# The first norm, the RG-LRU phase, the compressed scores and the S5 preparation of a two-block fp32 model, in another order

## The chip, the cores and the metric

The program runs on one core of a Trainium2 chip. The metric is the device time of one execution in microseconds (us). An execution is one launch that computes both blocks of the model for one sequence of 256 tokens.

## The reference, cut to what matters

Two model blocks of width 1024 are computed in fp32. The first is an RG-LRU layer with its feed-forward layer, then a sparse-attention (NSA) layer with its own. The second is a feed-forward layer, an S5 layer, two feed-forward layers around it and a block attention (MoBA) layer. The parts that the change touches:

```python
def rmsnorm(x, g):
    return x * lax.rsqrt(jnp.mean(x * x, axis=-1, keepdims=True) + EPS) * g

def rglru_mixer(h, ...):               # 1536 channels, T = 256
    u = h @ w_in
    xb, yb = u[..., :D_RNN], u[..., D_RNN:]
    xc = conv(xb, conv_w, width 4, causal) + conv_b
    r = sigmoid(blockdiag(xc, w_ra) + b_ra)
    i = sigmoid(blockdiag(xc, w_ix) + b_ix)
    log_a = -8 * r * softplus(-lam)
    a = exp(log_a); mult = sqrt(-expm1(2 * log_a))
    h_t = a_t * h_(t-1) + mult * i * xc   # scan over the 256 tokens
    return (hs * gelu(yb)) @ w_out

# NSA: scores of 16 heads (4 per key group) on the 15 compressed keys of each group
s_c = einsum('tghd,cgd->tghc', q, kc)
p_c = masked_softmax(s_c, mask_c)

# S5: tables from lam^k, B and C, which depend on no activation
y = einsum over (chunk kernel K, powers times B, powers times C)
```

## The kernel before

Everything is one instruction stream per engine, written out by hand. TensorE (PE) takes part in all of it: activations are held transposed, channels on partitions and the 256 tokens in the free dimension, and each weight matrix arrives in **halves** of 128x1024 (128x1408 in the down projections of the feed-forward layers). A half passes four engines:

- SP loads two halves at a time from HBM into one of 4 buffers `raw`.
- ACT copies a half to `w_hi`, a rounded version (`split_hi`, L846). It runs 4 halves ahead of PE (`SPLIT = 4`), because there are 4 buffers, and waits until PE has used the old one.
- DVE makes `w_lo = raw - w_hi` (`split_lo`, L1237).
- PE multiplies in three passes (L1970 to L1972), or in two wide ones (L1976, L1977) in the down and output projections.

The activations are split the same way into `hg_hi` (ACT, L849) and `hg_lo` (DVE, L1242). The norm's factor is applied behind the product: squares are summed, one PE product with a matrix of ones gives the mean (`mean_square`, L1989), ACT takes the root (L855) and DVE the reciprocal (L1247).

Each engine works through its own queue in order, and what stands where is set by tables of slots. In the RG-LRU phase slot `j` is one half of the input projection (24 halves: 0 to 11 give `xb`, 12 to 23 give `y`). The 1536 channels are worked in 4 groups `g` of 3 tiles. For each group come the convolution (`conv`, DVE, L1468 and L1470), the gates (PE, L2117), then sigmoids, exp, tanh and sqrt (ACT, L970 to L990, with three table loads) and the recurrence (DVE, L1489 to L1497). The tables `CONV_AT`, `GATES_AT`, `RECUR_AT` and `FINISH_AT` say in which slot each group's piece is written into each engine's queue, always behind that slot's own split. The gelu of `y` (ACT, L1006) follows a rule in the loop.

In the feed-forward phases slots 0 to 10 are pairs of hidden tiles (4 halves each) and slots 11 to 18 are the 8 tiles of the down projection (2 halves each). PE starts down tile `m` when tile `m - 2` has been added to `h` (`h_written`, L1264). Two feed-forward phases of the first block also carry the preparation of the S5 tables, in 8 portions of three pieces each. C makes `cp_s` (DVE, L1318 to L1322). K is PE's 16 small products L2097, which wait for it. B makes `ba_s` (DVE, L1332 to L1336). `C_AT`, `K_AT` and `B_AT` give the slots, first for the feed-forward phase at 181 to 383 us, then for the one at 640 to 838 us. ACT issues their DMAs: `s_ca`, `c_raw` and `b_raw` with K, and `s_ba`, `b_rows` and 8 times `l_rows` in the slot behind B.

```python
for j in range(2 * RT):                    # ACT, RG-LRU
    split_hi(half0 + j + SPLIT)
    ...
    if j in GATES_AT:
        gates(GATES_AT.index(j))           # sigmoids, exp, tanh, sqrt of group g
```

Of the kernel before, what the change touches and what calls it, by code (L numbers as in the profile page):

```python
# [31 lines left out]
ALU = mybir.AluOpType  # L32
# [6 lines left out]
P = 128  # L39
# [122 lines left out]
def two_blocks(nc, ins, out, phases):  # L162
# [4 lines left out]
    with ExitStack() as ctx:  # L167
# [74 lines left out]
        x_in = sem("x_in")  # L242
# [111 lines left out]
        kc_s = na.sb("kc_s", [P, NG * NC])  # L354
# [49 lines left out]
        gates_made = sem("gates_made")  # L404
        sc_done = sem("sc_done")
# [190 lines left out]
        def _(sp):  # L596
            def load(unit, it=0, row_step=0):
# [5 lines left out]
                src = ins[kind]  # L603
                if row_step:
# [29 lines left out]
        def _(pool):  # L634
# [176 lines left out]
            sum_squares(0, lambda m: pool.wait_ge(x_in, 16))  # L811
# [20 lines left out]
        def _(act):  # L832
            act.dma_start(vec[:, :], ins["vec"]).then_inc(consts_in, 16)
            act.dma_start(h[:, :, :], ins["x"]).then_inc(x_in, 16)


            def split_hi(half, it=0):
# [5 lines left out]
                act.wait_ge(raw_loaded[r], 16 * (half // (2 * RAW) + 1) + 16 * it)  # L843
# [115 lines left out]
            def rglru_phase(ph):  # L959
                half0 = 2 * ph["u0"]  # L960

                def gates(g):


                    r, i, rt = r_s[g % 2], i_s[g % 2], root_s[g % 2]
# [6 lines left out]
                    for q in range(GT):  # L972
                        n = GT + q
                        act.activation(i[:, q, :], bank[5 + n // 2][:, n % 2 * T:(n % 2 + 1) * T], ACT.Sigmoid,
                                       bias=gain("b_ix", GT * g + q)).then_inc(sigm_made, 1)
                    if g == 0:
                        act.wait_ge(sp4_made, 1)
# [20 lines left out]
                for j in range(2 * RT):  # L998
                    split_hi(half0 + j + SPLIT)
                    if j == 1:  # L1000
                        root(ph["norm"])
                    if j > RT and j % 2:
                        u = (j - RT) // 2
# [3 lines left out]
                    if j in GATES_AT:  # L1007
                        gates(GATES_AT.index(j))
# [48 lines left out]
            def nsa_phase(ph):  # L1057
# [7 lines left out]
                for j in range(52):  # L1065
# [15 lines left out]
                    if j >= 34 and j < 50 and j % 2:  # L1081
                        u = (j - 34) // 2
                        act.wait_ge(proj_read, base + 11 + u + 1)
                        act.activation(qr_s[0:96, 2 * u:2 * u + 2, :], q_s[0:96, 2 * u:2 * u + 2, :], ACT.Copy).then_inc(q_copied, 1)
                act.wait_ge(gate_lin, 2)
# [115 lines left out]
            act.wait_ge(x_in, 16)  # L1201
            act.wait_ge(consts_in, 16)
            for m in range(KT):
                make_hg_hi(phases[0]["gain"], m)
                if m == 0:
                    split_hi(0)
            for half in range(1, SPLIT):
                split_hi(half)
# [20 lines left out]
        def _(dve):  # L1229
# [206 lines left out]
            def softplus_lambda():  # L1436
# [19 lines left out]
            def rglru_phase(ph):  # L1456
                half0 = 2 * ph["u0"]

                def conv(g):

                    slot = GT * (g % 2)
                    for j in range(4):
                        for q in range(GT):
# [3 lines left out]
                            if j == 0:  # L1467
                                last = dve.tensor_scalar(o, x, gain("conv_0", m), gain("conv_b", m), ALU.mult, ALU.add)  # L1468
                            else:
                                last = dve.scalar_tensor_tensor(o, x, gain(f"conv_{j}", m), o, ALU.mult, ALU.add)  # L1470
# [34 lines left out]
                for j in range(2 * RT):  # L1505
                    split_lo(half0 + j + SPLIT)
                    if j == 1:
                        invert(ph["norm"])
                    if j < RT and j % 2:
# [104 lines left out]
            def nsa_phase(ph):  # L1614
# [23 lines left out]
                for j in range(52):  # L1638
# [48 lines left out]
                    if j == 38:  # L1687
                        dve.wait_ge(cmp_done, 1)
                        dve.tensor_copy(kc_s[0:96, :], bank[7][0:96, 0:NG * NC]).then_inc(cmp_kept, 1)
# [22 lines left out]
                for b in range(2):  # L1712
# [1010 lines left out]
```

## Time and profile before

| | before |
|---|---|
| time, median of 3 runs | 1889.27 us |
| lowest, highest | 1884.92, 1890.38 us |
| the profiled execution, timed | 1885.09 us |
| its span, first to last instruction | 1883.1 us |
| mean granted TensorE clock | 0.970 |
| PE busy | 1766.4 us (94%) |
| DVE busy | 1336.6 us (71%) |
| ACT busy | 857.2 us (46%) |
| POOL busy | 356.8 us (19%) |

The span is 2.0 us shorter than the time of the same execution. PE is busy for 94% of it, so what can be won or lost lies in the 117 us in which PE stands still, and in stretches in which its clock is at half speed. A queue entry of another engine matters only where PE waits for it.

### The profile page before, as it was taken

To read this page: it belongs to the slowest core of one execution; us is meant where nothing else is said; L and a number is where in the kernel's file an instruction comes from. 1 tells how busy PE (TensorE), PEld (TensorE's weight loads), DVE (VectorE), ACT (ScalarE), POOL (GpSimd) and SP (SyncE) were. 2 spreads that over 40 slices of the span, in tenths; PEclk is the share of its full clock that TensorE was granted. 3 is DMA by queue.
4 is the path that set the end of the run, shared out by engine and by line. 5 is a ranking of instruction groups with operands and counts; after the bars stand their busy time and mean duration, and the time that the engine had idled before them with its cause. 6 is when DMAs were issued, how large, how long until landed. Compare 5 with 4: busy or idle time off the path is not lost. (4 is left out here: it accounts for less than half of the span.)

```text
span 1883.1 us, 32526 instructions
## 1 busy us (share of the span) xinstructions
PE 1766.4 (94%) x13218; PEld 1673.2 (89%) x13218; DVE 1336.6 (71%) x1691; ACT 857.2 (46%) x1118; POOL 356.8 (19%) x327
## 2 busy tenths in 40 slices
PE   6959999997987999979999999999999999989999
PEld 6858998797976999869998888999899989879998
DVE  7877878788567777887875766666666665586663
ACT  4755444344346444434445325544354444355442
POOL 3223000206620300142002213000300035530000
PEclk9989999998979999999999999999999999999999
DMA  7225558456410467854564543556445644425561
GB/s 283 89 91 182 207 188 284 161 172 206 146 46 1 162 229 241 283 172 148 178 229 151 213 138 133 178 180 220 159 160 187 219 154 170 161 74 176 185 233 48
DMA packets 60795, 321.89 MB, mean 171 GB/s; under 512 B 7440, under 2 KB 20304, under 8 KB 30352
## 3 DMA queue, kind: packets, MB, share of 16 engines
q1 hardware_dynamic: 37296, 286.47, 42.9%
q10 hardware_dynamic: 18864, 21.74, 3.7%
q0 software_dynamic: 4528, 12.19, 1.9%
q8 instruction: 75, 1.23, 0.3%
q14 instruction: 32, 0.26, 0.0%
HBM read 309.16 MB, written 10.09 MB: 170 GB/s over the span
## 5 line engine op out<-in xcount | busy, mean ns | idle before, releaser
L1237 DVE TENSOR_TENSOR w_lo<-raw,w_hi 128x1024 fp32r<-128x1024 f32 (+2 forms) x516 | 683.8, 1330 | 332.0 <-ACT w_hi L846 330.6
L846 ACT ACTIVATE w_hi<-raw 128x1024 fp32r<-128x1024 f32 (+2 forms) x516 | 561.3, 1095 | 687.9 <-PE bank L1972 399.5
L1970 PE MATMUL bank<-hg_hi,w_hi 128*128 128x256 f32 (+1 forms) x2672 | 768.7, 288 | 41.0 <-DVE w_lo L1237 22.7
L1971 PE MATMUL bank<-hg_lo,w_hi 128*128 128x256 f32 (+1 forms) x2672 | 760.5, 285 | 0.0
L1972 PE MATMUL bank<-hg_hi,w_lo 128*128 128x256 f32 (+1 forms) x2672 | 760.4, 285 | 0.0
L1970 PEld LDWEIGHTS bank<-hg_hi,w_hi 128*128 128x128 f32 (+1 forms) x2672 | 514.4, 193 | 49.9 <-issue 16.5
L1971 PEld LDWEIGHTS bank<-hg_lo,w_hi 128*128 128x128 f32 (+1 forms) x2672 | 515.0, 193 | 0.3
L1972 PEld LDWEIGHTS bank<-hg_hi,w_lo 128*128 128x128 f32 (+1 forms) x2672 | 514.8, 193 | 0.0
L1976 PE MATMUL bank<-hid,w_hi 128*128 128x512 f32 x1056 | 375.2, 397 | 0.6 <-DVE hid L1388 0.4
L1977 PE MATMUL bank<-hid,w_lo 128*128 128x256 f32 x1056 | 300.1, 284 | 0.0
L1976 PEld LDWEIGHTS bank<-hid,w_hi 128*128 128x128 f32 x1056 | 200.1, 190 | 48.1 <-issue 1.0
L1977 PEld LDWEIGHTS bank<-hid,w_lo 128*128 128x128 f32 x1056 | 200.3, 190 | 0.0
L649 POOL TENSOR_TENSOR sumsq<-h 128x256 f32<-128x256 f32 x11 | 10.1, 915 | 879.8 <-DVE h L1264 868.2
L652 POOL TENSOR_TENSOR square<-h 128x256 f32<-128x256 f32 x77 | 87.3, 1134 | 227.9 <-DVE h L1264 226.9
L655 POOL TENSOR_TENSOR sumsq<-sumsq,square 128x256 f32<-128x256 f32 x77 | 90.2, 1172 | 6.0
L1242 DVE SCALAR_TENSOR_TENSOR hg_lo<-h,vec,hg_hi 128x256 fp32r<-128x256 f32 x80 | 67.1, 845 | 15.9 <-ACT hg_hi L849 15.9
L891 ACT ACTIVATE hid<-hid_f 128x512 fp32r<-128x512 f32 (+1 forms) x66 | 41.8, 633 | 59.9 <-DVE hid_f L1384 59.9
L887 ACT ACTIVATE silu_s<-gate_s 128x512 f32<-128x512 f32 x66 | 41.2, 624 | 60.3 <-DVE gate_s L1377 60.3
L1261 DVE SCALAR_TENSOR_TENSOR h<-bank,h 128x256 f32<-128x256 f32 x80 | 33.6, 420 | 48.5 <-PE bank L1977 48.1
L1381 DVE TENSOR_TENSOR up_s<-bank,rstd 128x512 f32<-128x512 f32 x66 | 45.4, 688 | 19.8 <-PE bank L1972 19.8
L1377 DVE TENSOR_TENSOR gate_s<-bank,rstd 128x512 f32<-128x512 f32 x66 | 45.4, 688 | 16.8 <-PE bank L1972 16.6
L849 ACT ACTIVATE hg_hi<-h,vec 128x256 fp32r<-128x256 f32 x80 | 39.6, 503 | 25.5 <-DVE h L1264 15.0
(377 smaller groups left out, 2017.7 us busy)
## 6 DMA issues: line engine op xcount, KB each, us to landing
raw<-in_w SPq DMA_DIRECT2D x187, 1024.0 KB, 4.8
raw<-in_w SPq DMA_DIRECT2D x48, 1408.0 KB, 6.1
raw<-in_q SPq DMA_DIRECT2D x14, 768.0 KB, 4.3
raw<-in_w SPq DMA_DIRECT2D x8, 768.0 KB, 4.2
b_rows<-in_s_b_rows ACTq DMA_DIRECT2D x8, 512.0 KB, 5.1
l_rows<-s_powers ACTq DMA_DIRECT2D x64, 64.0 KB, 6.0
s_ca<-cp_s ACTq DMA_DIRECT2D x8, 512.0 KB, 4.2
s_ba<-ba_s ACTq DMA_DIRECT2D x8, 512.0 KB, 3.0
```

The costliest lines, as they stand in the source:

```text
L652: pool.tensor_tensor(square[:, :], h[:, m, :], h[:, m, :], ALU.mult).then_inc(sq_step, 1)
L655: last = pool.tensor_tensor(sumsq[:, :], sumsq[:, :], square[:, :], ALU.add)
L846: act.activation(w_hi[s][:, 0:n], raw[r][:, c * n:(c + 1) * n], ACT.Copy).then_inc(hi_made, 1)
L1237: dve.tensor_tensor(w_lo[s][:, 0:n], raw[r][:, c * n:(c + 1) * n], w_hi[s][:, 0:n].bitcast(F32), ALU.subtract).then_inc(lo_made, 1)
L1242: dve.scalar_tensor_tensor(hg_lo[:, m, :], h[:, m, :], gain(gain_name, m), hg_hi[:, m, :].bitcast(F32), ALU.mult, ALU.subtract).then_inc(h ...
L1377: dve.tensor_tensor(two(gate_s[:, :]), two(gate[:, :]), twice(rstd), ALU.mult).then_inc(gate_scaled, 1)
L1381: dve.tensor_tensor(two(up_s[:, :]), two(up[:, :]), twice(rstd), ALU.mult).then_inc(up_scaled, 1)
L1970: pe.matmul(psum, w_hi_ap, x_hi_ap, start=first, stop=False, **kw)
L1971: pe.matmul(psum, w_hi_ap, x_lo_ap, start=False, stop=False, **kw)
L1972: return pe.matmul(psum, w_lo_ap, x_hi_ap, start=False, stop=last, **kw)
L1976: pe.matmul(psum[:, :].rearrange("p (a t) -> p a t", a=2), w_hi_ap, x_pair, start=first, stop=False)
L1977: return pe.matmul(psum[:, 0:T], w_lo_ap, x_pair[:, 0, :], start=False, stop=last)
```

## The change

1. **Start.** `vec` (all per-channel constants) is loaded first on SP's queue and no longer on ACT's. `x` and the first weight unit come in two parts each. ACT makes `w_hi` of half 0 ahead of the 8 `hg_hi`. The squares for the first norm are two ACT instructions into `y_gelu` instead of 15 POOL instructions, and PE sums them in 8 products instead of 1. The norm's root and reciprocal are written one slot earlier. DVE computes `softplus(-lam)` in two parts: the first ahead of everything else, the second in slot 2.
2. **RG-LRU.** The convolution's first tap goes from DVE to ACT (`first_tap`, slots `TAP_AT`), which needs no table. ACT's gate work is cut in two: `sigmoids` in the gates' slot and `decays` (exp, tanh, sqrt) one slot later. All tables of slots are new.
3. **Compressed scores.** 32 products with the queries as weights (N = 15) become 8 with the keys as weights (32 columns, N = 512, the four groups in the four column quarters of the array). Two ACT copies and 8 transposes follow.
4. **S5 preparation.** `C_AT`, `K_AT` and `B_AT` are new.

```diff
-CONV_AT = (3, 5, 10, 12)
-GATES_AT = (7, 10, 12, 15)
-RECUR_AT = (10, 12, 15, 21)
+TAP_AT = (3, 5, 9, 11)
+CONV_AT = (4, 6, 10, 12)
+GATES_AT = (6, 8, 12, 14)
+RECUR_AT = (11, 13, 16, 18)
+GELU_AT = {16: (0, 1), 17: (2,), 19: (3,), 21: (4,), 23: (5,)}
-C_AT = ((8, 11, 15), (1, 5, 9, 12, 15))
-K_AT = ((9, 12, 16), (2, 6, 10, 13, 16))
-B_AT = ((10, 13, 17), (3, 7, 11, 14, 17))
+C_AT = ((9, 12, 15), (1, 4, 7, 10, 14))
+K_AT = ((11, 14, 17), (3, 6, 9, 12, 16))
+B_AT = ((10, 13, 16), (2, 5, 8, 11, 15))
...
# ACT, RG-LRU
+                def first_tap(g):
+                    slot = GT * (g % 2)
+                    act.wait_ge(xb_made, (GT * g + GT + 1) // 2)
...
+                    for q in range(GT):
+                        act.activation(xc[:, slot + q, :], xb[:, slot + q, 1:1 + T], ACT.Identity, bias=gain("conv_b", GT * g + q),
+                                       scale=gain("conv_0", GT * g + q)).then_inc(tap_made, 1)
...
                 for j in range(2 * RT):
                     split_hi(half0 + j + SPLIT)
-                    if j == 1:
+                    if j == 0:
                         root(ph["norm"])
...
+                    if j in TAP_AT:
+                        first_tap(TAP_AT.index(j))
+                    if j in GATES_AT:
+                        sigmoids(GATES_AT.index(j))
+                    if j - 1 in GATES_AT:
+                        decays(GATES_AT.index(j - 1))
...
# ACT, start
-            act.wait_ge(x_in, 16)
+            split_hi(0)
...
+            split_hi(1)
+            for i in range(2):
+                act.activation(y_gelu[:, 4 * i:4 * i + 4, :], h[:, 4 * i:4 * i + 4, :], ACT.Square).then_inc(squares_made, 1)
...
# DVE, start and slot 2
+            softplus_lambda(0)
+            split_lo(0)
...
+                    if j == 2:
+                        softplus_lambda(1)
# PE, NSA
-                for b in range(2):
-                    for hd in range(NH):
-                        g = hd // 4
-                        last = pe.matmul(bank[7][:, NC * (NH * b + hd):NC * (NH * b + hd + 1)], q_s[0:96, hd, P * b:P * b + P],
-                                         kc_s[0:96, NC * g:NC * g + NC], start=True, stop=True)
...
+                for e in range(2):
+                    for g in range(NG):
+                        last = pe.matmul(bank[5 + e][32 * g:32 * g + 32, :].rearrange("p (i t) -> p i t", i=2), kc_s[0:96, 32 * g:32 * g + 32],
+                                         q_s[0:96, 4 * g + 2 * e:4 * g + 2 * e + 2, :], start=True, stop=True)
```

The rows below are queue entries of one engine in program order. A trailing number in `w_hi_56` to `w_hi_59` and `w_lo_60` to `w_lo_63` is the buffer, half 0 in the first of the four; `raw_52` to `raw_55` are the 4 load buffers.

**DVE, start of the RG-LRU phase.** Before, from the last entry of the softplus to the first group's convolution (`L1468`, `L1470`):

```order
L1454 TENSOR_SCALAR sp_71<-tiny_73 128x12
L1237 TENSOR_TENSOR w_lo_60<-raw_54,w_hi_56 128x1024
L1237 TENSOR_TENSOR w_lo_61<-raw_54,w_hi_57 128x1024
L1247 RECIPROCAL rstd<-rms 128x256
L1516 TENSOR_TENSOR xb<-bank,rstd 128x2x256
L1237 TENSOR_TENSOR w_lo_62<-raw_55,w_hi_58 128x1024
L1237 TENSOR_TENSOR w_lo_63<-raw_55,w_hi_59 128x1024
L1516 TENSOR_TENSOR xb<-bank,rstd 128x2x256
L1468 TENSOR_SCALAR xc<-xb,vec 128x256 x3
L1470 SCALAR_TENSOR_TENSOR xc<-xb,vec,xc 128x256 x9
```

After, from the middle of the softplus's second part to the same convolution (`L1512`), the splits being L1279 here:

```order
L1494 SCALAR_TENSOR_TENSOR tiny_73<-tiny_73,tiny_72 128x12 x7
L1495 SCALAR_TENSOR_TENSOR tiny_73<-tiny_73,tiny_75 128x12
L1496 TENSOR_SCALAR tiny_75<-vec 128x12
L1497 SCALAR_TENSOR_TENSOR tiny_73<-tiny_73,tiny_75 128x12
L1498 TENSOR_SCALAR sp_71<-tiny_73 128x12
L1279 TENSOR_TENSOR w_lo_63<-raw_55,w_hi_59 128x1024
L1560 TENSOR_TENSOR xb<-bank,rstd 128x2x256
L1279 TENSOR_TENSOR w_lo_60<-raw_52,w_hi_56 128x1024
L1512 SCALAR_TENSOR_TENSOR xc<-xb,vec,xc 128x256 x9
```

The second part of the softplus now stands between the splits of halves 6 and 7, behind the reciprocal, where before all of it stood ahead of the split of half 4. One split more (half 8, `w_lo_60<-raw_52`) stands ahead of the nine taps.

**ACT, RG-LRU slots 8 to 10.** Before, from the split of half 12 to that of half 15; half 14 is `w_hi_58<-raw_55`:

```order
L846 ACTIVATE w_hi_56<-raw_54 128x1024
L846 ACTIVATE w_hi_57<-raw_54 128x1024
L846 ACTIVATE w_hi_58<-raw_55 128x1024
L970 ACT_TABLE_LOAD
L970 ACTIVATE r_odd<-bank,vec 128x256 x3
L974 ACTIVATE i_odd<-bank,vec 128x256 x3
L983 ACT_TABLE_LOAD
L983 ACTIVATE rec_s<-r_odd,minus_sp_100 128x256 x3
L987 ACTIVATE r_odd<-r_odd,sp_71 128x256 x3
L990 ACT_TABLE_LOAD
L990 ACTIVATE root_odd<-r_odd 128x768
L846 ACTIVATE w_hi_59<-raw_55 128x1024
```

After, from the split of half 12 to that of half 14; L987 is the first tap of group 2, L998 and L1002 are the sigmoids of group 1, and L1016 to L1023 its exp, tanh and sqrt:

```order
L862 ACTIVATE w_hi_56<-raw_54 128x1024
L998 ACT_TABLE_LOAD
L998 ACTIVATE r_odd<-bank,vec 128x256 x3
L1002 ACTIVATE i_odd<-bank,vec 128x256 x3
L862 ACTIVATE w_hi_57<-raw_54 128x1024
L987 ACTIVATE xc<-xb,vec 128x256 x3
L1016 ACT_TABLE_LOAD
L1016 ACTIVATE rec_s<-r_odd,minus_sp_100 128x256 x3
L1020 ACTIVATE r_odd<-r_odd,sp_71 128x256 x3
L1023 ACT_TABLE_LOAD
L1023 ACTIVATE root_odd<-r_odd 128x768
L862 ACTIVATE w_hi_58<-raw_55 128x1024
```

The split of half 14 stood ahead of group 1's gate work and now stands behind all of it and behind the tap of group 2. DVE's convolution of group 2 stands behind the split of that same half in both.

**ACT, feed-forward phase with the first preparation, down tile 0 (slot 11).** Before; all DMA rows are issues:

```order
L849 ACTIVATE hg_hi<-h,vec 128x256
L955 DMA s_ba<-ba_s 128x1024
L919 DMA b_rows<-in_s_b_rows 128x1024
L923 DMA l_rows<-s_powers 32x512 x8
L846 ACTIVATE w_hi_58<-raw_53 128x1408
L846 ACTIVATE w_hi_59<-raw_53 128x1408
```

After:

```order
L865 ACTIVATE hg_hi<-h,vec 128x256
L960 DMA s_ca<-cp_s 1024x1x128
L925 DMA c_raw<-in_s_c 128x256
L926 DMA b_raw<-in_s_b 128x256
L971 DMA s_ba<-ba_s 128x1024
L935 DMA b_rows<-in_s_b_rows 128x1024
L939 DMA l_rows<-s_powers 32x512 x8
L862 ACTIVATE w_hi_58<-raw_53 128x1408
L862 ACTIVATE w_hi_59<-raw_53 128x1408
```

The three issues of K now stand in the same slot as the ten behind B (8 of them are `l_rows`), ahead of the two splits. The same nine rows stand in down tile 3 (slot 14), and such a row of issues in pairs 3, 6 and 9 and down tile 1 (slot 12) of the other preparing phase.

## Rows read from the trace of the kernel before

**Rows 1.** Waits of PE, 0 to 180 us: engine, line, releaser, total, times, longest
```profile
PE bank L1970 <- DVE w_lo L1237: 22.2, 4, 12.1
PE bank L1976 <- DVE y_gelu L1521: 11.4, 1, 11.4
```

**Rows 2.** Windows, 0 to 180 us: from:to, length, busy by engine, PEclk, DMA
```profile
114.50:118.50 4.00, 3.99 (x19) 4.00 (x20) 3.23 (x2) 0.82 (x3) 1.55 (x1) 0.50 0.14 16
118.50:122.50 4.00, 4.00 (x35) 4.00 (x35) 3.13 (x2) 2.53 (x3) 1.86 (x1) 0.99 0.50 184
```

**Rows 3.** Timeline of ACT, start: start us, us, what, [idle before]
```profile
24.14 1.06 ACT L846 ACTIVATE w_hi<-raw 128x1024 fp32r<-128x1024 f32 x1 [4.64 <-PE bank L1972]
...
37.88 1.06 ACT L846 ACTIVATE w_hi<-raw 128x1024 fp32r<-128x1024 f32 x1 [1.82 <-PE bank L1972]
```

**Rows 4.** Timeline of DVE, 20 to 45 us
```profile
27.26 0.17 DVE L1444 TENSOR_SCALAR tiny<-tiny 128x12 f32<-128x12 f32 x1
...
30.40 0.17 DVE L1454 TENSOR_SCALAR sp<-tiny 128x12 f32<-128x12 f32 x1
...
38.13 1.06 DVE L1468 TENSOR_SCALAR xc<-xb,vec 128x256 f32<-128x256 f32 x3
39.22 3.90 DVE L1470 SCALAR_TENSOR_TENSOR xc<-xb,vec,xc 128x256 f32<-128x256 f32 x9
```

**Rows 5.** Timeline of ACT, gates of group 1
```profile
66.60 1.28 ACT L983 ACT_TABLE_LOAD   x1
...
71.86 0.84 ACT L990 ACTIVATE root_odd<-r_odd 128x768 f32<-128x768 f32 x1
```

**Rows 6.** Waits of PE, preparing feed-forward phase, 181 to 383 us
```profile
PE bank L2097 <- issue: 6.3, 2, 3.6
```

**Rows 7.** Waits of PE, the other preparing phase, 640 to 838 us
```profile
PE bank L2097 <- issue: 4.2, 2, 2.8
```

**Rows 8.** Timeline of ACT, 318 to 334 us
```profile
324.67 0.54 ACTq L944 DMA_DIRECT2D s_ca<-cp_s  x1
...
325.95 0.92 ACTq L910 DMA_DIRECT2D b_raw<-in_s_b  x1
```

**Rows 9.** Timeline of ACT, 337 to 352 us
```profile
335.89 1.38 ACT L846 ACTIVATE w_hi<-raw 128x1408 fp32r<-128x1408 f32 x1 [2.08 <-PE bank L1977]
339.75 1.39 ACT L846 ACTIVATE w_hi<-raw 128x1408 fp32r<-128x1408 f32 x1 [2.48 <-PE bank L1977]
...
342.14 0.33 ACTq L955 DMA_DIRECT2D s_ba<-ba_s  x1
...
347.52 2.65 ACT L846 ACTIVATE w_hi<-raw 128x1408 fp32r<-128x1408 f32 x2 [4.88 <-PE bank L1977]
```

**Rows 10.** Timeline of DVE, 337 to 352 us
```profile
335.90 1.21 DVE L1332 TENSOR_TENSOR ba_s<-l_rows,b_rows 128x1024 f32<-128x1024 f32 x1
...
339.69 1.62 DVE L1237 TENSOR_TENSOR w_lo<-raw,w_hi 128x1408 fp32r<-128x1408 f32 x1
```

**Rows 11.** Timeline of DVE, 352 to 372 us
```profile
353.56 2.03 DVE L1318 TENSOR_TENSOR cp_tmp<-c_raw,pc_first 128x1280 f32<-128x1280 f32 x1
...
358.50 1.62 DVE L1237 TENSOR_TENSOR w_lo<-raw,w_hi 128x1408 fp32r<-128x1408 f32 x1
```

**Rows 12.** Lines of PE, 520 to 545 us: shapes, count, busy, mean ns, idle before
```profile
L2300 PE MATMUL bank<-kc_s,q_s 96*128 96x15 f32 x64 | 12.9, 357 | 1.3 <-DVE q_s L1699 1.3
...
L2331 PE MATMUL bank<-na_tab,score_c 128*128 128x128 f32 x8 | 2.0, 428 | 2.7 <-DVE score_c L1729 2.7
```

**Rows 13.** Timeline of DVE, 520 to 545 us
```profile
524.20 0.41 DVE L1702 TENSOR_TENSOR gate_f<-bank,rstd 48x256 f32<-48x256 f32 x1
...
533.88 0.84 DVE L1713 TENSOR_TENSOR score_c<-bank,na_tab 128x240 f32<-128x240 f32 x2
```

**Rows 14.** Timeline of PE, 355 to 360 us
```profile
358.69 1.08 PE L2097 MATMUL bank<-cp_s,b_raw 128*32 128x128 f32 x16 [3.58 <-issue]
```

**Rows 15.** Timeline of PE, 533 to 545 us
```profile
542.64 2.93 PE L2172 MATMUL bank<-ks_s,qr_s 96*128 96x256 f32 x6 [0.69 <-ACT prob_c L1094]
```

More of the change, by code:

```diff
@@ L241, in two_blocks @@
         consts_in = sem("consts_in")
-        x_in = sem("x_in")
+        x_in = [sem(f"x_in{i}") for i in range(2)]
+        first_half_in = sem("first_half_in")
+        squares_made = sem("squares_made")
+        tap_made = sem("tap_made")
         pool_const = sem("pool_const")
@@ L603, in load @@
                 src = ins[kind]
+                if unit == 0:
+                    half = size // 2
+                    sp.dma_start(raw[0][:, 0:half], src[row, :, 0:half]).then_inc(first_half_in, 16)
+                    sp.wait_ge(x_in[0], 16)
+                    sp.dma_start(raw[0][:, half:size], src[row, :, half:size]).then_inc(raw_loaded[0], 16)
+                    sp.wait_ge(x_in[1], 16)
+                    return
                 if row_step:
@@ L975, in gates, with decays @@
                                        bias=gain("b_ix", GT * g + q)).then_inc(sigm_made, 1)
+                def decays(g):
+                    r, rt = r_s[g % 2], root_s[g % 2]
                     if g == 0:
@@ L1461, in conv @@
                     slot = GT * (g % 2)
-                    for j in range(4):
+                    dve.wait_ge(tap_made, GT * g + GT)
+                    for j in range(1, 4):
                         for q in range(GT):
@@ L1466, in conv @@
                             o = xc[:, slot + q, :]
[L1467 to L1470, printed above, removed]
+                            last = dve.scalar_tensor_tensor(o, x, gain(f"conv_{j}", m), o, ALU.mult, ALU.add)
                             if q < GT - 1:
@@ L1984, in mean_square, with first_mean_square @@
             def mean_square(norm):
-                pe.wait_ge(sumsq_made, norm + 1)
-                if norm == 0:
-                    pe.wait_ge(pool_const, 2)
+                pe.wait_ge(sumsq_made, norm)
                 pe.matmul(bank[NORM_BANK][:, 0:T], ones_d[:, :], sumsq[:, :], start=True, stop=True).then_inc(ms_made, 1)
+            def first_mean_square():
+                pe.wait_ge(pool_const, 2)
+                for k in range(KT):
+                    if k % 4 == 0:
+                        pe.wait_ge(squares_made, k // 4 + 1)
+                    last = pe.matmul(bank[NORM_BANK][:, 0:T], ones_d[:, :], y_gelu[:, k, :], start=k == 0, stop=k == KT - 1)
+                last.then_inc(ms_made, 1)
             def from_hg(half, psum, it=0, hg=None, cols=P):
@@ L2306, in nsa_phase @@
                 last.then_inc(gate_turned, 1)
+                pe.wait_ge(sc_rows_kept, 2)
+                for b in range(2):
+                    for i in range(4):
+                        last = pe.transpose(bank[(7, 3)[b]][:, P * i:P * i + P], sc_rows[:, i // 2, i % 2, P * b:P * b + P],
+                                            na_tab[:, 3 * T:3 * T + P])
+                last.then_inc(sc_done, 1)
                 att = Attention("nsa")
```

77 lines of the change are left out of this document (41 added, 36 removed).

## The prediction

> **What bounds the kernel now.** I read the waits of PE stretch by stretch first, since PE is busy for nearly the whole span: only what PE waits for counts, and only the four stretches that the change touches can move. In the RG-LRU phase PE waits 22.2 us for `w_lo`, of which 12.1 is the start of the program, and 11.4 us once for the last `y_gelu` [rows 1]. The windows show the price of a long wait besides the wait itself: behind the one that ends at 114.5 us the granted clock is 0.50, its lower level of 1.2 GHz, for 4 us and PE begins 19 products there; in the next 4 us, at 0.99, it begins 35 [rows 2]. So a wait of some microseconds costs about 2 us more behind it. In the two preparing phases PE waits at the small products of K, which need `cp_s`: 6.3 us in two waits [rows 6] and 4.2 in two [rows 7]. In NSA the 64 records of the compressed scores hold PE for 12.9 us [rows 12]. The timelines of ACT and DVE then give the durations for the chains below. One half takes PE 2.88 us in the RG-LRU phase (an ACT split of 1.06 us after 1.82 us idle) [rows 3] and 3.86 us in a down projection (the splits at 335.89 and 339.75) [rows 9].
>
> **Start.** Half 1 ended at 24.14 us, where its buffer was split again [rows 3], so two halves took 12.0 us for the 5.8 of full rate: POOL's squares ran beside DVE's splits, and the clock fell. Without them, with `w_hi` first in ACT's queue and the load in two parts, I put the first product at 11.4 (12.1 before), half 0 at 5.0 us (low clock), 8 fp32 products for the mean square at 0.44 each (0.49 for 256 columns at low clock [rows 15]; I take a little less), and half 1 at 2.9: half 2 starts at 22.8 instead of about 24.5. The softplus no longer stands ahead of the split of half 4, which ends one of the three short `w_lo` waits. Start: -1.5 us, between -3 and +1.
>
> **RG-LRU, group 0.** The second part of the softplus costs DVE 3.3 us (27.26 to 30.57) [rows 4] and now stands ahead of the splits of halves 7 and 8 and of the convolution. Half 2 ends at 25.7, its buffer's split on ACT at 26.8, on DVE (1.62 for 1408 columns [rows 10], so 1.2 for 1024) at 28.0; softplus to 31.3; half 7 to 32.5; `xb` (512 elements, half of the 1.21 for 1024 [rows 10]) to 33.1; first tap on ACT, 1.3, to 34.4; `w_hi` and `w_lo` of half 8 to 36.7; nine taps, 3.9 [rows 4], to 40.6. PE is at these gates behind half 6, at 22.8 + 5 x 2.88 = 37.2: a new wait of 3.4 us. The tap takes 1.06 us off DVE [rows 4], less than the softplus puts in.
>
> **RG-LRU, group 2.** This is the largest term. The nine taps of group 2 stand behind the split of half 14, and that split now stands behind group 1's sigmoids, the first tap of group 2 and group 1's exp, tanh and sqrt. The latter took 6.1 us (66.60 to 72.70) [rows 5]: two table loads of 1.28, the root of 0.84, and 0.45 for each of six others. From the end of gates(1) on PE: sigmoids 2.7, `w_hi` of half 13 1.06, `w_lo` 1.2, `xb` 0.6, tap 1.3, decays 6.1, `w_hi` of half 14 1.06, `w_lo` 1.2, nine taps 3.9: 19.1 us, and a little more beside POOL's work. PE reaches gates(2) after four halves, 11.5 us. The new wait is 8 us (7.5 to 9). Before, the split of half 14 stood ahead of all this.
>
> In the second half of the phase the decays and recurrences, one slot further back, hold up splits of halves 20, 21 and 23 by 2.0, 5.8 and 3.7 us when I follow the queues on with these durations, and the last `y` by 5.7. That is about 29 us of waits behind the start, for 10.1 (the `w_lo` waits without the start) + 11.4 + some 2 now: +6. There are five waits of over 3 us instead of two, and 3 x 1.7 us of low clock: +5. With the start this part gives **+9.5 us**, between -1 (the tail swallows group 2's wait) and +14.
>
> One rule is weighed here. The row has a table load at 1.28 us, and six activations and the root fill the rest of the 6.1 us [rows 5]. The Trainium skill (ScalarE: Activation LUTs, What ACT_TABLE_LOAD costs) counts about 1.4 us of drain on top of each load; two loads would then make the decays 8.9 us and the wait for gates(2) some 3 us longer. The row has no room for it, and the row decides.
>
> **First preparing phase.** K's three issues take ACT 2.2 us (324.67 to 326.87) [rows 8], those behind B 5.4 (342.14 to 347.52, where the next split starts) [rows 9]. Now they stand together: 7.6 us in slots 11 and 14, ahead of the splits for the next tile but one. DVE writes a tile's `h` between those two splits, and PE starts the next tile but one on it. So the chain from one write of `h` to the next is: in a slot with the block 0.4 + 7.6 + 1.4 (`w_hi` [rows 9]) + 1.6 (`w_lo` [rows 10]) + 0.9 (two adds) = 11.9; with C 0.8 + 2 x 1.6 + 4.9 (353.56 to 358.50 [rows 11]) + 0.9 = 9.8; with B, 3.8 (335.90 to 339.69 [rows 10]), 8.7. Slots 11 to 14 hold block, C, B and block: 42.3 us for four tiles of 7.72. The write at 342.1 was 5.4 us ahead of its use at 347.5 [rows 9]. 42.3 - 30.9 - 5.4 = 6 us of new waits for `h`. The remaining slots (C, B, K) add 3 that end at the next phase's first activation, and the pairs with C and B side by side 2. The two waits of 6.3 us [rows 6] go, since K stands two or three slots behind C; long waits and their low clock are as many as before. 11 - 6.3 gives **+4.5**, between -8 (nothing comes back, and 2 us of clock are saved) and +9.
>
> **Second preparing phase.** The block stands in pairs 3, 6 and 9 (slot 12 has room). ACT can split a buffer when PE leaves it, three halves (8.6 us) before it is needed, and the two splits take 2.3: 6.3 us to spare. A block of 5.4 fits, one of 7.6 is 1.3 late, and B's 3.8 us or C's 4.9 on DVE in the slot beside it can come on top. I take 3.3 for each of the three, 10; less 4.2 [rows 7]: **+5.5**, between 0 (3 x 1.3) and +11.
>
> **Compressed scores.** Eight products of the new form, each in a quarter of the array's columns: the nearest row is L2097, also in column quarters, 16 of 128 columns in 1.08 us [rows 14], so 0.27 for 512 columns and 2.2 for all. If they don't run beside each other: six of 256 columns took 2.93 [rows 15], so 7.8 for eight of 512. The first now starts at 533.9 - 0.5 - 12.9 = 520.4 (the mask's add is at 533.88 [rows 13], the turn of the gates 0.5). After: 522.6, two copies on ACT 1.2, meanwhile `gate_f` at 524.6 [rows 13], which is late next, its turn 0.4, eight transposes 2.0 [rows 12]: 527.0 instead of 533.8. **-7 us**; without overlap 531.2, -2.5. The masked copy of the keys is one DVE pass earlier in the phase, beside other work: nothing, or 0.5.
>
> **Sum:** 9.5 + 4.5 + 5.5 - 7 = +12.5 on the profiled execution: 1885.1 + 12.5 = 1897.6 us (span 1895.6). The median of the runs lies 4.2 above that execution and the lowest run at it; I add 2.4: **1900 us**.
>
> **Rivals.**
> *Forecast, 0.58:* gates(2) and the block of issues are waited for; 1893 to 1908.
> *No overlap in the scores, 0.08:* the keys as weights gain 2.5 instead of 7; 1904.5. The products L2097 speak against it [rows 14].
> *Faster, 0.19:* ACT's look-ahead covers the issue block. It decides at 6.3 us: below that, `w_lo` comes in time and the waits for `cp_s` go with nothing in their place. For it: the 5.4 us block of now brings PE no wait, and eight issues in a row need not cost the same next to three others. The two phases then give -10.5 - 4 of clock, NSA -7, RG-LRU +9.5 less what the tail gives back: -12, 1873 on the profiled execution and 1876 in the median; against it, the 7.6 is a sum of measured issue times.
> *No change, 0.15:* the RG-LRU tail swallows half of its new waits (it waits 11.4 us for the last `y` today, and an earlier delay only moves that), the two preparing phases cost 5 together: 4 + 5 - 7 = +2, 1889.
>
> A measurement of this kernel tells about 0.3%, 5.7 us, from no change. Slower holds 0.58 + 0.08, same 0.15, faster 0.19. The range reaches into the faster case, 1876, and to 1910 above (upper bounds of one preparing phase and RG-LRU together); the forecast's own is 1893 to 1908.
>
> **What would show it.** Waits of PE at the gates (L2168 after) near 40 us, about 3.5, and near 80 us, about 8, for `xc`; none of L1976 for `y_gelu` over 7. No waits of K's products in the preparing phases, but waits at the wide passes of about 4 us near slot 14 with DVE's splits idle for 7 us behind ACT, and `w_lo` waits in the pairs of the second. In NSA the mask's add comes about 6.6 us behind the first product of the scores, now 13.5. The forecast is wrong if ACT's issues take under 6.3 us together, if DVE reaches the taps of group 2 before PE, or if an interval of low clock opens where I count none.

## The result and the profile after

| | before | changed |
|---|---|---|
| time, median | 1887.10 us (4 runs) | 1909.49 us (4 runs) |
| lowest, highest | 1883.93, 1890.38 us | 1905.11, 1912.48 us |
| the profiled execution, timed | 1885.09 us | 1912.43 us |
| its span | 1883.1 us | 1910.6 us |
| mean granted TensorE clock | 0.970 | 0.966 |

The change makes the kernel slower: ratio 1.0107, 95% interval 1.0091 to 1.0124, so about 20 us (17 to 23), and 22.4 between the medians. The forecast was 1900 us, 13 more than the median of before. The measured median lies 9.5 above it, 1.5 above the forecast's own range (1893 to 1908) and just inside the whole one, which ended at 1910. The profiled execution of before was 2 us under its median and that of the changed kernel 3 us over, so the two traces show 27.5 us, more than the change itself.

The page of the changed kernel, busy time by engine:

```profile
PE 1772.5 (93%) x13192; PEld 1675.9 (88%) x13192; DVE 1325.2 (69%) x1680; ACT 863.9 (45%) x1133; POOL 342.6 (18%) x312
```

POOL and DVE have less to do. PE is still busy 6.1 us longer with the same projections, and stands still 21.4 us longer.

Where the time went is read from the products with the matrix of ones that open each norm. They mark the ends of the phases:

| phase ends (next norm's product) | before | changed | phase longer by | forecast |
|---|---|---|---|---|
| start and RG-LRU | 181.1 | 192.7 | +11.6 | +9.5 |
| first preparing feed-forward phase | 383.5 | 402.2 | +7.1 | +4.5 |
| NSA | 640.5 | 653.0 | -6.2 | -7 |
| second preparing feed-forward phase | 837.7 | 863.8 | +13.6 | +5.5 |
| all that follows | | | +1.4 | 0 |

These are two single executions. The traces of the experiments below show how far a phase moves by itself. With the old preparation tables the second preparing phase lasts 196.7 to 203.9 us in eight traces (mean 200.9), and before's 197.2 is the second shortest. With the new ones it lasts 210.8 here and 207.5 in e3_prep. Against the mean the change costs some 8 us there, not 13.6. For the first preparing phase the same comparison gives +7.2 (208.6 for 201.4).

The waits of PE in the changed kernel's first phase (engine, line, releaser: total, times, longest), for [rows 1] of before:

```profile
PE bank L2168 <- DVE xc L1512: 13.2, 2, 9.7
PE bank L2014 <- DVE w_lo L1279: 11.5, 3, 5.4
PE bank L2014 <- DVE hg_lo L1284: 11.3, 2, 10.5
PE bank L2020 <- DVE y_gelu L1565: 4.8, 1, 4.8
```

The 11.4 us for the last `y_gelu` are 4.8, and at the gates (L2168) PE waits 13.2 us, for 2.4 before. Behind the start there are six waits of 2 us and more where there were two.

**The gates of group 2.** The timeline of ACT in the changed kernel, then that of DVE, then of PE (start, length, what, [idle before]):

```profile
61.55 1.21 ACT L998 ACTIVATE r_odd<-bank,vec 128x256 f32<-128x256 f32 x3
62.63 1.22 ACT L1002 ACTIVATE i_odd<-bank,vec 128x256 f32<-128x256 f32 x3
63.80 1.06 ACT L862 ACTIVATE w_hi<-raw 128x1024 fp32r<-128x1024 f32 x1
67.50 1.59 ACT L987 ACTIVATE xc<-xb,vec 128x256 f32<-128x256 f32 x3 [2.64 <-DVE xb L1560]
69.11 1.28 ACT L1016 ACT_TABLE_LOAD   x1
...
74.36 0.84 ACT L1023 ACTIVATE root_odd<-r_odd 128x768 f32<-128x768 f32 x1
75.11 1.99 ACT L862 ACTIVATE w_hi<-raw 128x1024 fp32r<-128x1024 f32 x2
```

```profile
66.79 0.68 DVE L1560 TENSOR_TENSOR xb<-bank,rstd 128x512 f32<-128x512 f32 x1
76.19 1.99 DVE L1279 TENSOR_TENSOR w_lo<-raw,w_hi 128x1024 fp32r<-128x1024 f32 x1 [8.72 <-ACT w_hi L862]
78.10 3.89 DVE L1512 SCALAR_TENSOR_TENSOR xc<-xb,vec,xc 128x256 f32<-128x256 f32 x9
```

```profile
82.04 4.21 PE L2168 MATMUL bank<-xc,gate_w 128*128 128x256 f32 x9 [9.70 <-DVE xc L1512]
```

Read from ACT down to PE, these three are one chain. ACT splits half 13, waits 2.64 us for `xb`, makes the tap, then exp, tanh and sqrt until 75.2, and only then splits half 14 (75.11). DVE stands idle for 8.72 us for that split, then makes `w_lo` and the nine taps, and PE starts the gates at 82.04 after 9.70 us of waiting.

The windows behind that wait (length, busy by engine, PEclk) show its second price:

```profile
82.00:86.00 4.00, 3.96 (x9) 3.19 (x10) 3.93 (x5) 2.24 (x4) 0.00 (x0) 0.50 0.37 113
86.00:90.00 4.00, 4.00 (x18) 3.48 (x17) 3.90 (x7) 0.56 (x2) 0.00 (x0) 0.91 0.35 150
```

At 0.50 PE begins 9 records of the gates' products in 4 us. (A group's 14 fp32 products are 28 records, two each.) At 1.00 it begins 20 such records in 4 us, as e4_start (described below) shows:

```profile
84.00:88.00 4.00, 4.00 (x20) 3.54 (x19) 3.93 (x3) 1.22 (x1) 1.61 (x1) 1.00 0.00 0
```

PE is busy all the while: low clock doesn't show as a wait.

**The preparing phases.** ACT in down tile 3 (slot 14) of the first one, DVE behind it, and PE:

```profile
360.86 0.68 ACTq L925 DMA_DIRECT2D c_raw<-in_s_c  x1
...
362.52 0.48 ACTq L971 DMA_DIRECT2D s_ba<-ba_s  x1
...
363.51 5.83 ACTq L939 DMA_DIRECT2D l_rows<-s_powers  x8
369.44 2.64 ACT L862 ACTIVATE w_hi<-raw 128x1408 fp32r<-128x1408 f32 x2 [8.64 <-issue]
```

```profile
370.85 1.62 DVE L1279 TENSOR_TENSOR w_lo<-raw,w_hi 128x1408 fp32r<-128x1408 f32 x1 [8.05 <-ACT w_hi L862]
...
372.84 0.42 DVE L1306 SCALAR_TENSOR_TENSOR h<-bank,h 128x256 f32<-128x256 f32 x1
```

```profile
373.32 0.75 PE L2020 MATMUL bank<-hid,w_hi 128*128 128x512 f32 x1 [5.03 <-DVE h L1306]
```

The ten issues behind B follow those of K without a gap. The 13 issues take 9.0 us here (360.30 to 369.34), for 7.6 in the forecast: `l_rows` took 5.83, where the row of before behind the 5.4 had 4.43. Both splits of the tile wait behind it, then DVE (8.05 us idle), then PE (5.03 us), which may not start the next tile but one before `h` is written. In the second phase the blocks of pairs 3, 6 and 9 take 8.8, 9.5 and 9.9 us, and PE then waits 3.7, 2.3 and 4.7 us for `w_lo`. The waits of PE there, and windows around two of them:

```profile
PE bank L2014 <- DVE w_lo L1279: 7.9, 4, 3.7
PE bank L2020 <- DVE w_lo L1279: 4.7, 1, 4.7
```

```profile
710.00:720.00 10.00, 7.77 (x43) 7.80 (x44) 8.54 (x9) 5.99 (x7) 0.00 (x0) 0.66 0.81 241
...
790.00:800.00 10.00, 5.80 (x18) 4.93 (x19) 6.95 (x7) 6.04 (x6) 0.00 (x0) 0.66 0.71 249
```

Those three are 10.7 of the 12.6 us, and the 4.2 of [rows 7] are gone. All waits of the phase together grew from 8.9 to 16.0 us. The rest of the 13.6 us is the clock: over that phase the mean granted clock was 1.00 before and is 0.96 now. In windows of half a us, PE is busy for 14.8 us at the lower level, where before it was for none. But e4_start, with the old tables, has 9.5 us of it there, so not all of this comes from the new tables.

**The scores.** Lines of PE, 530 to 565 us (count, busy, mean ns, idle before), for [rows 12] and [rows 14]:

```profile
L2385 PE MATMUL bank<-na_tab,score_c 128*128 128x128 f32 x8 | 2.0, 428 | 4.9 <-DVE score_c L1776 4.9
L2348 PE MATMUL bank<-q_s,prob 96*32 96x512 f32 x16 | 1.9, 596 | 1.3 <-DVE q_s L1745 1.3
```

The 8 products (16 records; `prob` holds the keys) take 1.9 us, where the 64 records of before took 12.9. The forecast had 2.2 from L2097, and 7.8 if they did not run beside each other. At the clock of 1.00, the 16 records of 512 columns start 0.12 us apart, where e4_start's 20 records of 256 columns took 0.20 each. The Trainium skill (TensorEngine Tiling (Array Packing), Key Properties) says that different tiles of the array can work in parallel; this row agrees.

Part of the gain is the clock. The old products ran at the lower level for most of their time, though PE was busy without a gap. The windows over them, before and changed:

```profile
520.34:531.31 10.97, 10.97 (x56) 10.97 (x57) 2.78 (x3) 3.69 (x4) 10.18 (x10) 0.55 0.57 196
...
538.72:540.65 1.93, 1.92 (x16) 0.47 (x16) 0.43 (x1) 1.93 (x3) 1.65 (x2) 1.00 0.61 166
```

All ten traces with the old form have 0.53 to 0.70 there, and all four with the new one 1.00.

### The profile page after: what moved, and what is told of

The parts are those of the page before. It is cut to its first block and busy times, and to the rows that moved or that the text cites. A ratio compares the mean times of both kernels' runs of the same rounds, so it can differ in the third digit from the quotient of the medians.

```text
span 1910.6 us, 32466 instructions
## 1 busy us (share of the span) xinstructions
PE 1772.5 (93%) x13192; PEld 1675.9 (88%) x13192; DVE 1325.2 (69%) x1680; ACT 863.9 (45%) x1133; POOL 342.6 (18%) x312
## 5 line engine op out<-in xcount | busy, mean ns | idle before, releaser
L1279 DVE TENSOR_TENSOR w_lo<-raw,w_hi 128x1024 fp32r<-128x1024 f32 (+2 forms) x516 | 684.0, 1329 | 384.0 <-ACT w_hi L862 382.1
L669 POOL TENSOR_TENSOR sumsq<-sumsq,square 128x256 f32<-128x256 f32 x70 | 81.4, 1162 | 5.5
L1284 DVE SCALAR_TENSOR_TENSOR hg_lo<-h,vec,hg_hi 128x256 fp32r<-128x256 f32 x80 | 62.8, 793 | 6.3 <-ACT hg_hi L865 6.3
L1419 DVE TENSOR_TENSOR gate_s<-bank,rstd 128x512 f32<-128x512 f32 x66 | 45.4, 688 | 16.8 <-PE bank L2016 16.6
```

What stands on the lines that cost most here:

```text
L669: last = pool.tensor_tensor(sumsq[:, :], sumsq[:, :], square[:, :], ALU.add)
L1279: dve.tensor_tensor(w_lo[s][:, 0:n], raw[r][:, c * n:(c + 1) * n], w_hi[s][:, 0:n].bitcast(F32), ALU.subtract).then_inc(lo_made, 1)
L1284: dve.scalar_tensor_tensor(hg_lo[:, m, :], h[:, m, :], gain(gain_name, m), hg_hi[:, m, :].bitcast(F32), ALU.mult, ALU.subtract).then_inc(h ...
L1419: dve.tensor_tensor(two(gate_s[:, :]), two(gate[:, :]), twice(rstd), ALU.mult).then_inc(gate_scaled, 1)
```

## The experiments

Each was timed in five rounds against the kernel before on the same chip: e1 to e4 and e9 to e12 on one chip, e5 to e8 on another. The change in us is (ratio - 1) x 1888, with the interval. Differences of 3 or 4 us between two experiments lie within these intervals.

| kernel | median us | ratio (95%) | us on before |
|---|---|---|---|
| e1_start_rglru: parts 1 and 2 | 1897.00 | 1.0051 (1.0031 to 1.0071) | +9.6 (6 to 13) |
| e4_start: part 1 | 1884.39 | 0.9981 (0.9969 to 0.9992) | -3.6 (-6 to -2) |
| e2_scores: part 3 | 1883.40 | 0.9974 (0.9964 to 0.9984) | -4.9 (-7 to -3) |
| e3_prep: part 4 | 1901.33 | 1.0072 (1.0053 to 1.0090) | +13.6 (10 to 17) |
| e5_prep_apart | 1872.03 | 0.9912 (0.9891 to 0.9933) | -16.6 (-21 to -13) |
| e6_prep_few_issues | 1877.97 | 0.9950 (0.9931 to 0.9968) | -9.4 (-13 to -6) |
| e7_decays_later | 1896.38 | 1.0036 (1.0019 to 1.0053) | +6.8 (4 to 10) |
| e8_softplus_later | 1894.64 | 1.0031 (1.0016 to 1.0046) | +5.9 (3 to 9) |
| e10_both_later | 1891.00 | 1.0017 (1.0004 to 1.0029) | +3.2 (1 to 5) |
| e11_tap_on_dve | 1895.10 | 1.0031 (1.0013 to 1.0049) | +5.9 (2 to 9) |
| e9_best_of | 1865.96 | 0.9875 (0.9860 to 0.9890) | -23.6 (-26 to -21) |
| e12_after_mended | 1873.19 | 0.9906 (0.9886 to 0.9926) | -17.8 (-21 to -14) |

**The parts alone.** e1, e2 and e3 are the change without the other parts; e4 has the new start, and `root(ph["norm"])` at `j == 0`, but the old gates, taps and RG-LRU tables.

> The start and the RG-LRU phase as changed (parts 1 and 2), scores and S5 preparation as before. In the trace of the changed kernel the phase ends 11.6 us later than before (192.7 for 181.1 at the next norm's product). If the parts add up (my theory), this kernel takes +11 to +12 us on the kernel before, with the two waits at the gates of 3.5 and 9.7 us. Rival: part of the loss is given back later in the program (a late phase is only shifted, the loads and splits behind it have more time), then it is under +8.

> The start alone (part 1: loads in halves, w_hi first, squares on ACT, mean square in 8 products, root and reciprocal one slot earlier, softplus in two parts), with the RG-LRU tables, gates and first tap as before. My theory says that the start is worth a little and the queue order of the RG-LRU phase costs it all: -2 us on before (between -4 and +1), so that the RG-LRU tables cost 13 to 14. Rival: the second part of the softplus, now behind the split of half 6, holds up the first convolution in the old tables too; then +2 to +4, and the RG-LRU tables cost only 8 to 10.

> The compressed scores with the keys as weights alone (part 3). In the trace of the changed kernel the stretch from the NSA phase's norm to the next norm is 6.2 us shorter. Theory: the eight products run beside each other in the array's column quarters, -6 to -7 us on before. Rival: most of the 6.2 came from other splits and clock windows of a shifted schedule; then between -3 and 0 here.

> The tables of the S5 preparation alone (part 4). In the trace of the changed kernel the two preparing phases take 7.1 and 13.6 us longer. Theory: ACT's block of issues with its late splits, and the low clock behind each wait: +18 to +21 us on before. Rival: the 13.6 of the second phase comes partly from where the earlier loss put its clock and its loads; then +10 to +15.

The parts add up: 9.6 - 4.9 + 13.6 = +18.3 for the +20 of the whole (17 to 23). e1's +9.6 lies between its theory (+11 to +12) and its rival (under +8). The start is worth 3.6, so the RG-LRU order costs 13.2, and the rival by which the softplus's second part is what hurts in any table is out. The scores gained 4.9, between the theory and its rival, with an interval that reaches to 6.8. The preparation cost 13.6, less than the theory's 18 and inside the rival's 10 to 15. The theory had taken the 13.6 us of one trace's second phase for the change's own. e3's trace has +10.3 there against the trace of before, and about +6.6 against the mean of the eight with the old tables. So the part beyond that is not shown to come from the change, nor from its coming late.

**What in the preparation costs.** Two ways to shorten the block, with the change's tables otherwise:

```diff
# e5_prep_apart, on e3_prep
-B_AT = ((10, 13, 16), (2, 5, 8, 11, 15))
+B_AT = ((11, 14, 17), (3, 6, 9, 12, 16))
# e6_prep_few_issues, on e3_prep
                 for part in range(2):
-                    for row in range(LC):
-                        powers = lp_dram[part, ST * row + 4 * kt:ST * row + 4 * kt + 4, :].rearrange("a n -> (a n)")
-                        act.dma_start(l_rows[32 * row:32 * row + 32, part, :], powers[None, :].broadcast_to([32, 4 * P])).then_inc(b_in, 16)
+                    powers = lp_dram[part].rearrange("(r s) n -> r s n", s=ST)[:, 4 * kt:4 * kt + 4, :].rearrange("r a n -> r (a n)")
+                    act.dma_start(l_rows[:, part, :], powers[:, None, :].broadcast_to([LC, 32, 4 * P])).then_inc(b_in, 16)
...
-                dve.wait_ge(b_in, 16 * 9 * (kt + 1))
+                dve.wait_ge(b_in, 16 * 3 * (kt + 1))
```

> The new S5 preparation tables alone, but B in K's slot, (11, 14, 17) and (3, 6, 9, 12, 16), so that ACT's issues behind B come one slot after those of K, as before, while K still stands two or three slots behind C. Theory (the joined block of 12 issues, 7.6 us, makes the splits late): no wait of PE of over 1 us in the preparing phases and none for K's products, -8 to -14 us on before. Rival (C next to B or B next to C on DVE makes w_lo and h late): waits of 1 to 4 us stay at the same places, +5 us or more.

> The new S5 preparation tables alone, with the 8 issues of l_rows per portion written as 2 (all four rows of powers in one). The tables and DVE's work are those of the change; only ACT's block shrinks, from 7.6 us to about 4. Theory: below 6.3 us it is covered; -8 to -14 us on before. Rival (DVE's order): the waits stay, +8 to +13 as the tables alone.

Both turn a loss of 13.6 us into a gain, e6 within its theory and e5, at -16.6, beyond the -8 to -14 expected. (The joined block has 13 issues, not 12.) PE's waits in the first preparing phase, of e5 and then of e6:

```profile
PE bank L1976 <- DVE w_lo L1237: 0.6, 1, 0.6
PE bank L1976 <- DVE hid L1388: 0.5, 1, 0.5
PE bank L1970 <- DVE hg_lo L1242: 0.3, 1, 0.3
```

```profile
PE bank L1969 <- DVE hg_lo L1241: 3.5, 1, 3.5
PE bank L1975 <- DVE h L1263: 1.8, 2, 1.0
```

In e5 nothing is left of the 6.3 us of [rows 6], no new wait is longer than 0.6 us here and 1.3 in the second phase (but for the norm's, as before), and the granted clock is 1.00, its upper level, through both phases. In e6 ACT's block here is 5.1 us long, of which two issues of `l_rows` take 1.81 (4 rows of powers in one, 0.9 each, where eight single ones took 4.4 to 5.8):

```profile
342.55 0.57 ACTq L943 DMA_DIRECT2D s_ca<-cp_s  x1
...
345.82 1.81 ACTq L922 DMA_DIRECT2D l_rows<-s_powers  x2
347.73 2.65 ACT L846 ACTIVATE w_hi<-raw 128x1408 fp32r<-128x1408 f32 x2 [4.68 <-PE bank L1976]
```

That is under the 6.3 us at which the forecast let it decide, and the waits behind blocks are gone but for 1.8 us. In the pairs of the second phase e6's blocks take 5.2 to 6.5 us and bring no wait over 1.5.

Where waits begin can be read from one block that all kernels but e6 have alike: `c_raw`, `b_raw`, `b_rows` and 8 `l_rows`, some 10 us into the second preparing phase. The same 11 issues took ACT a different time in each trace, and PE's next wait for `w_lo` follows:

| trace | ACT's block | PE waits | difference |
|---|---|---|---|
| before | 5.58 us | 0.3 us | 5.3 |
| changed | 6.83 | 1.5 | 5.3 |
| e4_start | 8.02 | 2.7 | 5.3 |
| e7_decays_later | 8.77 | 3.5 | 5.3 |

The nine other traces lie on the same line: the wait is the block less 5.3 us, within 0.1. So ACT may be away for 5.3 us there, not 6.3. The blocks of pairs 3, 6 and 9 in the changed kernel left 5.2, 7.1 and 5.2. This block also explains a part of what the second phase moves by itself: before's 197.2 us go with the shortest one, e7's 203.9 with the longest. Why the same issues take 5.6 us once and 8.8 another time is not shown.

The wait of 3.5 us at the end of the first phase stays. There C, B and K stand in slots 15, 16 and 17, and in e6's trace DVE works from 357 to 371 us without a gap; e5, with B one slot later, doesn't have it. So the block explains most of the loss and the rival (C and B side by side on DVE) a smaller part: e6 is 7 us behind e5, and 6.4 of that in the first phase (199.8 for 193.4).

**What in the RG-LRU order costs.** Three moves, on e1:

```diff
# e7_decays_later: group 1's exp, tanh, sqrt from slot 9 to 10
+DECAYS_AT = (7, 10, 13, 15)
-                    if j - 1 in GATES_AT:
-                        decays(GATES_AT.index(j - 1))
+                    if j in DECAYS_AT:
+                        decays(DECAYS_AT.index(j))
# e8_softplus_later
-                    if j == 2:
-                        softplus_lambda(1)
...
                         conv(g)
+                        if g == 0:
+                            softplus_lambda(1)
# e11_tap_on_dve
-                    if j in TAP_AT:
-                        first_tap(TAP_AT.index(j))
...
-                    for j in range(1, 4):
+                    for j in range(4):
```

> Start and RG-LRU as changed, with the exp, tanh and sqrt of group 1 one slot later (slot 10), behind the split of half 14 on which the convolution of group 2 stands. Start and RG-LRU as changed took +9.6 us on before. Theory: the wait at the gates of group 2 falls from 9.7 to about 2 and its low clock goes: +0 to +3 on before. Rival: the chain of decays and recurrences sets the end of the phase, the wait returns at the last halves or the last y: +6 to +10.

> Start and RG-LRU as changed, with the second part of the softplus behind the first convolution (slot 4) instead of in slot 2. Theory: the wait of 3.5 us at the gates of group 0 goes, with 2 us of low clock: +4 to +6 us on before instead of +9.6. Rival: the next wait, at the gates of group 2, takes it up: +8 to +10.

> Start and RG-LRU as changed (+9.6 us), with both moves: the exp, tanh and sqrt of group 1 behind the split of half 14 (alone: +6.8) and the second part of the softplus behind the first convolution (alone: +5.9). Theory: the gains of 2.8 and 3.7 add, +2 to +4. The rest against the start alone (-3.7) is then the taps and the second half of the phase. Rival: one chain of ACT and DVE through the whole phase, so that the two gains are the same one: +5 to +7.

> Start and RG-LRU as changed (+9.6 us), with the first tap of the convolution back on DVE. Theory: ACT no longer waits for xb ahead of group 1's exp, and 12 taps cost DVE 1.1 us more; the wait at the gates of group 2 falls from 9.7 to 7 or so, +6 to +9. Rival: DVE is the scarce engine in this phase and the tap on ACT is what the new order gains: +11 to +15.

e7 took the wait at the gates of group 2 from 9.7 to 2.8 us, but brought a new one of 3.3 at those of group 3. Its +6.8 is in the range of its rival, 2.8 us better than e1 and not the 7 or more expected. e8, at +5.9, is where its theory had it, though the wait at the gates of group 0 fell only from 3.5 to 2.1. Each of these gains alone is within the noise of the timings; together, in e10, they are 6.4 us and clear of it (+3.2, 1 to 5, for +9.6, 6 to 13). The ends of the phase in the traces say the same: 191.4 us in e1, 188.9 in e7, 189.5 in e8 and 186.3 in e10. With the tap back on DVE (e11) the phase ends at 186.9, with 6.6 instead of 9.7 us at the gates of group 2, and the kernel takes +5.9. So the rival by which the tap on ACT spares a scarce DVE falls, and the tap on ACT seems to cost some us, how much the timings don't resolve. What is left in e10 against e4 is 6.8 us. Their waits, e10 first:

```profile
PE bank L2006 <- DVE hg_lo L1279: 11.3, 2, 10.5
PE bank L2006 <- DVE w_lo L1274: 9.8, 3, 5.4
PE bank L2160 <- DVE xc L1507: 7.9, 4, 3.3
PE bank L2012 <- DVE y_gelu L1558: 4.8, 1, 4.8
```

```profile
PE bank L1991 <- DVE y_gelu L1539: 11.7, 1, 11.7
PE bank L1985 <- DVE hg_lo L1256: 11.4, 2, 10.5
PE bank L1985 <- DVE w_lo L1251: 9.1, 1, 9.1
PE bank L2139 <- DVE xc L1486: 2.4, 2, 1.8
```

Behind the start that is 9.8 + 7.9 + 4.8 and 11.7 + 9.1 + 2.4: 22.5 and 23.2 us. The sums are about equal, but e10 spreads them over eight waits, and of e4's four two hold nearly all. The windows from the first half to the next norm (e10, then e4):

```profile
12.00:186.00 174.00, 150.66 (x937) 139.04 (x937) 127.34 (x173) 101.37 (x144) 39.58 (x28) 0.91 0.42 154
```

```profile
12.00:177.00 165.00, 140.82 (x934) 131.82 (x934) 133.93 (x185) 96.64 (x133) 40.59 (x28) 0.93 0.45 163
```

PE does the same work in 150.7 and in 140.8 busy us. Most of the difference is the clock. In windows of half a us, PE is busy at the lower level for 25.0 us in e10 and for 9.1 in e4; at half speed those 15.9 us cost 8.0 of the 9.8. In e10 the clock is 0.72 on average around each of the first three waits. In e4 part of the low stretches falls into the two long waits and costs nothing there. That it is the number of waits which makes this difference is my reading; no run isolates it.

**The best of them.** e9 has the start, the scores and e5's tables, with the RG-LRU phase as before. e12 is the whole changed kernel with the moves of e5, e7 and e8.

> The parts that gained by themselves, together: the new start, the compressed scores with the keys as weights, and the new S5 preparation tables with B in K's slot; the RG-LRU phase as before. Alone they took -3.8, -4.8 and -16.8 us on before. Theory: they add up, -22 to -27 us. Rival: the gains of separate stretches partly fall into each other through the clock or the loads: -15 to -20.

> The whole changed kernel with three moves: B in K's slot, group 1's exp, tanh and sqrt behind the split of half 14, the second part of the softplus behind the first convolution. Theory: the sum of the parts, +3 (RG-LRU and start) - 4.8 (scores) - 16.8 (preparation), -16 to -21 us on before, and behind the best of the parts by what the RG-LRU order still costs. Rival: a late RG-LRU phase takes part of it, -10 to -14.

e9 is the fastest kernel of this study: 1865.96 us, 23.6 under before, where the parts alone sum to -3.6 - 4.9 - 16.6 = -25.1. e12 has -17.8 for 3.2 - 4.9 - 16.6 = -18.3.

## Why the prediction was right, and where its sizes were off

By the timings the sum +12.5 became +18.3 to +20: RG-LRU with the start 9.6 for 9.5, the preparation 13.6 for 10, the scores -4.9 for -7.

- **Direction and mechanisms.** Slower, as forecast, by the places named: gates of group 2, gates of group 0, the block of issues. The faster rival, at 0.19, named the point that decides, a block of 6.3 us. The block was forecast at 7.6, measured at 8.6 to 9.9, and where e6 made it 5.1 to 6.5, the kernel was faster than before. The point itself lay 1 us too high where the runs measure it (5.3). The size was too small: +12.5 for about +20, and the median lies above the forecast's own range.
- **Start: -1.5 forecast, -3.6 measured** (e4, and the phase's end in its trace 3.5 earlier). The first product came at 10.5 us, not 11.4, and from 12 to 24 us the mean granted clock was 1.00 (0.86 before) where the forecast had half 0 at the low one.
- **RG-LRU, waits.** At the gates of group 0, 3.5 us for 3.4. At those of group 2, 9.7 for 8: `w_lo` took 2.0 us, not 1.2, twice, at 64.90 and 76.19, each time with a product of POOL running (63.93 and 75.28). In the second half of the phase 2.3, 5.4, 3.9 and 4.8 for 2.0, 5.8, 3.7 and 5.7. The order's whole cost was 13.2 for 11. That the start and this term together came out at 9.6 for 9.5 is in part luck: each was off by some 2 us, with opposite signs.
- **First preparing phase: +7.1 for +4.5.** The new waits are 13.6 us (8.6 for `h`, 3.8 for `hg_lo`, 1.2 others) for 11. The blocks are longer than the forecast's 7.6: 8.6 us in slot 11 and 9.0 in slot 14.
- **Second preparing phase: +13.6 in this trace, +8 against the mean of the old tables, for +5.5.** This is the term most off in size. "I take 3.3 for each of the three, 10; less 4.2": the three waits were 10.7. That is near 10 partly by luck. The forecast made up its 3.3 from a block 1.3 us over its 6.3 and DVE's work beside it; measured, the blocks were 2.5 to 3.6 us over it, and e6, with short blocks and the same work on DVE, has only waits up to 1.5 there. What the sum left out is the low clock behind each wait, which the same prediction had counted, at 1.7 to 2 us a wait, in the RG-LRU phase. The three stretches are 14.8 us of busy PE at half speed, some 7 us. "An interval of low clock opens where I count none" was one of the prediction's own signs of being wrong, and here it came.
- **Scores: -7 forecast, -6.2 in the trace, -4.9 by itself.** The two prices of the products, 2.2 and 7.8 us, hold only by luck. The forecast took records for products: 16 records of L2097 are 8 products, and 6 of [rows 15] are 3. It also took both rows as they are, at a clock of 0.50. The two slips cancel, since the new products ran at 1.00. The NSA phase lasts 257.0 us on average in the ten traces with the old scores and 252.0 in the four with the new ones, 5 less. The products overlap and `gate_f` is late next (a wait of 2.4 us at its turn), both as said. That PE then waits longer for `score_c` was left out: 4.9 us for the 2.7 of [rows 12].
- **The rivals.** "The products of the scores don't overlap" is out by their row. "The tail swallows half" is out: the waits of the tail are there in full (16.4 us from 119 us on, for 17.2 forecast). The no-change sum counted on it.

The rule on the table load (ScalarE: Activation LUTs, What ACT_TABLE_LOAD costs, in the Trainium skill) would have given a wait at group 2's gates some 3 us longer. In the changed kernel the load at 69.11 took 1.28 us and exp, tanh, load and sqrt were over at 75.2, 6.1 us after it began: as before, with no room for a drain.

## What to carry to other kernels

An engine that converts weights ahead of PE has a budget in time: how long it may be away before a split is late (three halves less the two splits by the forecast, 6.3 us; 5.3 where it could be measured). Add up every piece that a slot table puts between two splits, DMA issues included, against that budget. Two pieces that each fit may not fit together, and one slot's distance was worth 30 us here (e3 against e5). Most waits also cost low clock behind them, so count waits, not only their sum, and count them in every phase. And before a single trace's phase is given a cause, see how much that phase moves between traces in which nothing was changed there.

## What the runs showed that was not expected

- The granted clock fell to its lower level while PE was busy throughout, in the 64 records of 15 columns of the old scores. In e5_prep_apart they start at 511.1 us; the clock is 1.00 from 512 to 514, 0.81 to 516 and 0.50 to 520, with PE busy in all of it.
- DMA issues on ACT take as long as compute: 0.48 to 0.81 us for each of the eight 64 KB `l_rows` (3.87 to 6.50 for the eight, before and changed), 8.6 to 9.9 us for the blocks of thirteen named above in the changed kernel. Four of them written as one took 0.9 in e6's row above.
- PE waits of equal sum (22.5 and 23.2 us) stood beside 9.8 us more busy time of PE when they came in eight pieces than in four, two of them long.
- A wait of the same length is not followed by the same clock each time. The wait for K's products near 792 us was 2.85 us in the kernel before, with 1.00 around it, and 2.88 in e4, where the phase is unchanged, with 0.50 to 0.71 from 792 to 800 us. That phase took 5.8 us longer there, with a wait of 2.7 us for `w_lo` near 659 us besides. The wait of 1.80 us at the gates is the opposite case: 0.50 behind it in the kernel before (89 to 91 us), 1.00 in e4 (82 to 90 us).
